# Regrouping the weight sums and the factor terms of a fast-matrix-product feed-forward stage

## The chip, the cores and the metric

The kernel runs on one core of one Trainium2 chip. TensorE (PE in the profile; PEld is its weight load), VectorE (DVE), ScalarE (ACT), GpSimd (POOL) and SyncE (SP) run in parallel and meet through semaphores only; sixteen DMA engines move data between SBUF and device memory. The metric is the device time of the kernel in microseconds (us), as the median of several executions.

## The reference

One decoder layer is applied to a prompt of 1024 tokens and to 8 single sample tokens, all with 1024 features in float32:

```python
x = x + W_out [conv(h); gla(h)],   h = rms_norm(x) @ w_in      # conv taps and a gated linear attention
x = x + cross_attn(rms_norm(x), memory K, V)                   # 4 heads, 256 memory tokens
x = x + relu(rms_norm(x) @ w_up) ** 2 @ w_down                 # 1024 -> 4096 -> 1024
y = rms_norm(x)
```

The outputs are y, the states of the convolution and of the linear attention, and the memory's keys and values. The change touches the last matrix products (w_up and w_down), what prepares them, and the times at which some transfers for them are made.

## The kernel before

Features lie on the 128 partitions, and the T = 1032 tokens along the free dimension. Every product is made in three matmuls of rounded parts (high by high, high by low, low by high), so each weight block needs a "high" copy, made by ScalarE, and a "low" rest, made by VectorE or GpSimd, and so does each moving operand.

**Tiles.** The program is numbered in weight tiles t: 16 for the memory's keys and values, 21 for the input projection (from T_IN = 16), 8 for the output projection (T_OUT = 37), 8 for the queries (T_XQ = 45), and from T_XO = 53 those of the attention's output: two over all tokens, then twelve half tiles (XO_HALVES), six for the tokens of half 0 and six for half 1. `load_w` (line 635) loads one weight tile of 512 KB on SP's queue, `w_high` (L1022) and `lo` (L902) split it. The half tiles' matmuls are at L2205; `residual_half` on VectorE (L2845) adds the result to x in `x_res` and frees the PSUM bank; its counterpart on ScalarE (L1494) squares it and `square_half` (L2851) adds the square to the norm's sum. The bank of half tile j is used again by half tile j + 2.

**Steps.** The feed-forward stage is 64 steps s: half 0 of the tokens in steps 0 to 31, half 1 in 32 to 63; within a half four groups of 4 up steps and 4 down steps. A step is a product of 2 x 2 blocks by the fast scheme with seven products instead of eight (L2264): 84 matmuls of 128x258. Its seven weight operands are A11, A12, A22 and four sums S1 to S4 of weight blocks. The moving operand has seven parts too: four quarter blocks B and three combinations T. For up steps they are the "factors" in `u_f32`/`u_op`: `factors(half, k)` scales x by the norm (two instructions, L2858) and makes the combinations (L2860, L2861, L2862), `factor_high` on ScalarE (L1519) and `factor_rest` on VectorE (L2866) split them. For half 0 they are made between the half tiles; for half 1 in steps 28 to 31 (SWITCH = 28), the last down steps of half 0.

**Weight pairs.** Two weight operands make a pair j of 512 KB. `load_pair` (L794, SP's queue) loads it into a ring of six; it waits until the product that last used the place is done. ScalarE (`comb_top`, L1527) and VectorE (`low_pair`, L2875) split it. Per step there are 3.5 pairs.

**Sums.** The sums S1 to S4 are made by DMA in device memory: SP copies a block, a GpSimd-issued DMA adds another to it (accumulate). The eight groups g have 1 MB for each sum. Groups 0 to 5 are made between tiles, from `SUM_START`, by `copy_sums` (L658, L660, L663, L666) and `add_sums` (L910, L913, L916, L919). Groups 6 and 7 ("late") are made in pieces of 256 KB in the steps that `LATE_SUMS` names: for each group six rows, (copy of S1 and S3, their add, copy of S2, add, copy of S4, add), each with the step of its four pieces. SP's copies (L674, L675, L679, L683) stand behind its pair loads, which the products release; GpSimd's adds (L986, L987, L991, L995) wait only for the first copy phase:

```python
if phases[1][p] == s:
    if p == 0:
        wait_copied(gp, g, 8)
    gp.dma_start(sum_piece(g, "S1", p), block_piece(g, "A21", p), accum_op=ALU.add)...
```

Group g is used in steps 4g to 4g + 3 and again 32 steps later. In each step ScalarE first does the rest of the step before, then `copy_first` (L1535, after the step's first product; the fifth product waits for it), then the step's comb_tops. Each engine does its instructions in order.

## Time and profile before

| what | value |
|---|---|
| time, median of 3 runs | 1449.14 us (1445.93 to 1452.72) |
| the profiled execution's own time | 1448.39 us |
| its span, first to last instruction | 1446.7 us |
| mean granted TensorE clock | 0.984 of full speed |
| PE busy | 1378.8 us, 95% |
| DVE busy | 1035.6 us, 72% |
| ACT busy | 743.3 us, 51% |
| POOL busy | 317.3 us, 22% |
| DMA | 268.25 MB, 185 GB/s in the mean |

The span is 1.7 us shorter than the execution's time; differences in the span are taken as differences in the time. A busy PE is modelled, so the lost time is better read from the length of a step than from PE's busy share: step s begins where ScalarE's `copy_first(s)` starts, step 0 at 739.2 us, step 28 at 1048.4, step 32 at 1103.4 and step 56 at 1346.1.

A row of the windows view gives a stretch, its length in us, then the busy us (and number of instructions) of PE, PEld, DVE, ACT and POOL, and last the granted clock, the DMA engines' busy share and GB/s.

### The profile page before, as it was taken

The page shows a single profiled execution, that of the slowest core. Times are in us where ns is not written, and L with a number is a line of the kernel's source. Part 1 is how long each engine was busy: PE and PEld are TensorE (multiplying, and loading weights), DVE is VectorE, ACT ScalarE, POOL GpSimd, SP SyncE. Part 2 cuts the span into 40 slices and gives each one's busy share as a digit, 9 for nine tenths or more (in the row PEclk, how much of TensorE's full clock was granted, in tenths as well). Part 3 has the DMA queues.
Part 4 walks back from the last instruction along what each step waited for, and adds up shares of the span by engine and source line. Part 5 has one row for each costly group of instructions (what it writes and reads, how often), then busy time and mean ns, then how long its engine had stood idle before and what let it go on. Part 6 is the DMA issues. An engine that isn't in the chain of part 4 may idle for free.

```text
span 1446.7 us, 25804 instructions
## 1 busy us (share of the span) xinstructions
PE 1378.8 (95%) x10477; PEld 1341.1 (93%) x10477; DVE 1035.6 (72%) x1403; ACT 743.3 (51%) x1063; POOL 317.3 (22%) x264
## 2 busy tenths in 40 slices
PE   7899999999999899999999989989997999999997
PEld 7799999998999899979898889989987999999997
DVE  5619999886533455624887678776898888798884
ACT  7561254448523333413465465554745757575674
POOL 6736495125342111104401010100000000000000
PEclk9999999999999999999999899999999999999998
DMA  9976796562595822493158788777544555666652
GB/s 355 306 173 204 174 162 150 154 121 74 198 301 179 235 74 63 153 361 117 59 190 220 232 236 238 233 209 217 180 160 132 183 183 164 199 194 210 198 167 60
DMA packets 137093, 268.25 MB, mean 185 GB/s; under 512 B 16840, under 2 KB 31496, under 8 KB 135312
## 3 DMA queue, kind: packets, MB, share of 16 engines
q1 hardware_dynamic: 119696, 233.04, 49.3%
q0 software_dynamic: 17280, 33.56, 13.3%
q8 instruction: 84, 1.38, 0.4%
q14 instruction: 33, 0.27, 0.1%
HBM read 254.26 MB, written 79.41 MB: 231 GB/s over the span
## 4 chain that ended last, share of the span: by engine, by line
PE 67%; DVE 15%; DMA 7%; ACT 6%; issue 3%; POOL 1%; SPq 0%; DVEq 0%; ACTq 0%; POOLq 0%
PE ps L2264 29%; DVE ps L2477 7%; PE ps L1806 6%; PE ps L1693 6%; PE ps L2100 6%; PE m L2264 5%; DMA raw_a<-sums 3%; PE ps L2205 3%; DMA w_raw<-in_wt 2%; PE m L1774 2%; PE ps L2134 1%; PE ps L2053 1%; PE m L2013 1%; DVE u_f L2858 1%; DVE u_op L2866 1%
## 5 line engine op out<-in xcount | busy, mean ns | idle before, releaser
L902 POOL TENSOR_TENSOR w_split<-w_raw,w_split 128x512 fp32r<-128x512 f32 x114 | 161.4, 1467 | 392.5 <-ACT w_split L1022 392.4
L1806 PE MATMUL ps<-a_op,w_split 128*128 128x344 f32 x1440 | 235.2, 323 | 4.0 <-ACT a_lr L1160 4.0
L1806 PEld LDWEIGHTS ps<-a_op,w_split 128*128 128x128 f32 x1440 | 229.1, 190 | 4.6 <-ACT a_lr L1160 4.2
L1527 ACT ACTIVATE comb_a<-raw_a 128x1024 fp32r<-128x1024 f32 x148 | 153.4, 1053 | 117.1 <-DMA raw_a<-in_wt 73.0
L2264 PE MATMUL ps<-d_op,comb_a 128*128 128x258 f32 x1512 | 196.4, 287 | 9.9 <-ACT p L1535 4.9
L2264 PE MATMUL ps<-u_op,comb_a 128*128 128x258 f32 x1512 | 191.6, 284 | 14.3 <-DVE u_op L2866 5.4
L2264 PEld LDWEIGHTS ps<-d_op,comb_a 128*128 128x128 f32 x1512 | 189.5, 192 | 12.7 <-issue 6.8
L2264 PEld LDWEIGHTS ps<-u_op,comb_a 128*128 128x128 f32 x1512 | 185.7, 190 | 16.7 <-issue 6.6
L2875 DVE TENSOR_TENSOR comb_a<-raw_a,comb_a 128x1024 fp32r<-128x1024 f32 x148 | 179.8, 1219 | 1.8 <-ACT comb_a L1527 1.7
L2477 DVE SCALAR_TENSOR_TENSOR ps<-conv_in,par,ps 128x1024 f32<-128x1024 f32 x103 | 133.0, 1291 | 3.3
L1693 PE MATMUL ps<-a_op,w_split 128*128 128x344 f32 x576 | 91.5, 320 | 0.0
L1693 PEld LDWEIGHTS ps<-a_op,w_split 128*128 128x128 f32 x576 | 90.6, 188 | 0.5 <-issue 0.5
L1022 ACT ACTIVATE w_split<-w_raw 128x1024 fp32r<-128x1024 f32 x58 | 61.0, 1052 | 51.9 <-PE ps L2205 22.4
L2100 PE MATMUL ps<-b_op,w_split 128*128 128x344 f32 x504 | 83.0, 321 | 0.0
L2100 PEld LDWEIGHTS ps<-b_op,w_split 128*128 128x128 f32 x504 | 79.7, 188 | 0.4
L2205 PE MATMUL ps<-a_op,w_split 128*128 128x258 f32 x576 | 72.5, 288 | 4.8 <-DVE x_res L2845 4.8
L2205 PEld LDWEIGHTS ps<-a_op,w_split 128*128 128x128 f32 x576 | 71.6, 194 | 5.5 <-DVE x_res L2845 5.4
L2958 DVE TENSOR_TENSOR d_op<-d_f,d_op 128x1806 fp32r<-128x1806 f32 (+2 forms) x40 | 63.7, 1609 | 6.4 <-ACT d_op L1569 6.4
L1527 ACT ACTIVATE comb_b<-raw_b 128x1024 fp32r<-128x1024 f32 (+1 forms) x38 | 39.6, 1041 | 44.5 <-DMA raw_b<-in_wt 23.0
L1569 ACT ACTIVATE d_op<-d_f 128x1806 fp32r<-128x1806 f32 (+2 forms) x40 | 53.9, 1368 | 12.2 <-DVE d_f L2948 12.2
L2264 PE MATMUL ps<-u_op,comb_c 128*128 128x258 f32 x396 | 51.0, 283 | 1.0 <-ACT p L1535 0.6
L2264 PE MATMUL ps<-u_op,comb_b 128*128 128x258 f32 x396 | 51.6, 285 | 0.0
(367 smaller groups left out, 2357.5 us busy)
## 6 DMA issues: line engine op xcount, KB each, us to landing
raw_a<-sums SPq DMA_DIRECT2D x167, 256.0 KB, 3.0
raw_a<-in_wt SPq DMA_DIRECT2D x129, 256.0 KB, 3.0
w_raw<-in_wt SPq DMA_DIRECT2D x59, 512.0 KB, 4.4
sums<-in_wt POOLq DMA_DIRECT2D x24, 1024.0 KB, 13.9
sums<-in_wt SPq DMA_DIRECT2D x12, 1024.0 KB, 10.0
sums<-sums SPq DMA_DIRECT2D x12, 1024.0 KB, 6.6
raw_c<-sums SPq DMA_DIRECT2D x43, 256.0 KB, 3.0
raw_b<-sums SPq DMA_DIRECT2D x42, 256.0 KB, 3.0
```

The lines of the kernel that those rows point to most:

```text
L902: gp.tensor_tensor(split(t, slot)[:, 1, part, :], src, split(t, slot)[:, 0, part, :].bitcast(F32), ALU.subtract).then_inc(w_low_done, 1)
L1022: act.activation(split(t, slot)[:, 0, :, :], src, ACT.Copy).then_inc(w_high_done, 1)
L1527: act.activation(pair_of(j)[0][:, 0:n_, 0], pair_of(j)[1][:, 0:n_, 1], ACT.Copy).then_inc(comb_high, 1)
L1569: act.activation(d_op[:, m, 0, f, :], d_f32[:, m, 1, f, :], ACT.Copy).then_inc(factors_high, 1)
L1693: last = pe.matmul(ps[:, c0 // CB, 0:w], w_split[:, slot, wp, k, :], src[:, k, xp, c0:c0 + w], start=(k == 0 and j == 0), stop=(k == KT - ...
L1806: last = pe.matmul(PS[0][:, b, 0:CB], w_split[:, p % 2, wp, k, :], a_op[:, k, xp, b * CB:(b + 1) * CB], start=(k == 0 and j == 0), stop=(k ...
L2100: last = pe.matmul(PS[0][:, b, 0:CB], w_split[:, t % 2, wp, k, :], b_op[:, k, xp, b * CB:(b + 1) * CB], start=(k == 0 and j == 0), stop=(k ...
L2205: last = pe.matmul(PS[bank_of(t)][:, b, 0:Q], w_split[:, t % 2, wp, k, :], a_op[:, k, xp, c0:c0 + Q], start=(k == 0 and i == 0), stop=(k = ...
L2264: last = pe.matmul(SETS[s % 2][BANK[i]][:, 0:Q], weights[:, wp, k, :], op[:, k, xp, FACTOR[i], :], start=(i < 4 and k == 0 and j == 0), st ...
L2477: link(dve.scalar_tensor_tensor(out=conv_acc, in0=src, scalar=t_, in1=conv_acc, op0=ALU.mult, op1=ALU.add))
L2875: dve.tensor_tensor(c[:, 0:n_, 1], raw_[:, 0:n_, 1], c[:, 0:n_, 0].bitcast(F32), ALU.subtract).then_inc(comb_low, 1)
L2958: dve.tensor_tensor(d_op[:, m, 1, f, :], d_f32[:, m, 1, f, :], d_op[:, m, 0, f, :].bitcast(F32), ALU.subtract).then_inc(factors_low, 1)
```

## The change

It has four parts.

1. Groups 0 to 4 of the sums are begun 3 tiles later (`SUM_TIMES` in place of `SUM_START`), group 5 up to 11 tiles later, its last add at t = 64.
2. GpSimd waits, in every step of half 0, for that step's first product before it issues its adds; before, all adds of a phase could go as soon as its copies had landed. The steps of the late groups are set anew. Both groups' first copies are now in steps 1 to 4.
3. The factors of half 1 are made early and kept in device memory. SP saves half 1 of x (`spill_rows`, before and in step 0). VectorE scales x in place in steps 6, 7, 13 and 14 (`scale_half`) and makes the combinations into `spare` in steps 15, 21, 22 and 23 (`terms_of`). ScalarE's queue stores the seven parts in the step after each (`store_terms`, four DMAs). SP loads them into `u_f32` at steps 28 and 29 (`load_terms`) ahead of these steps' pair loads, and loads x again ahead of those of step 31. `factors(1, k)` goes; `factor_high(1, 3)` moves from step 32 to 31; `factor_rest(1, k)` stays.
4. Between the half tiles, `residual_half(j)` stands ahead of `factors(0, k)` on VectorE and of `factor_high` on ScalarE from j = 7 on; `low_pair(2)` and `comb_top(2)` stand one place earlier.

```diff
@@ -100,9 +100,12 @@
-SUM_START = [T_IN - 6 + 6 * g for g in range(6)]
-LATE_SUMS = {6: ((0, 1, 2, 3), (4, 5, 6, 7), (8, 9, 10, 11), (12, 13, 14, 15), (16, 16, 17, 17), (19, 19, 20, 20)),
-             7: ((4, 5, 6, 7), (8, 9, 10, 11), (12, 13, 14, 15), (16, 17, 18, 19), (20, 20, 21, 21), (23, 23, 24, 24))}
+SUM_TIMES = [[T_IN - 3 + 6 * g + d for d in (0, 1, 2, 3, 7, 8, 12, 13)] for g in range(5)]
+SUM_TIMES.append([T_XQ + 5, T_XQ + 6, T_XQ + 7, T_XQ + 8, T_XO + 4, T_XO + 6, T_XO + 9, T_XO + 11])
+SCALE_AT = (6, 7, 13, 14)
+TERMS_AT = (15, 21, 22, 23)
+LATE_SUMS = {6: ((1, 2, 3, 4), (5, 6, 7, 8), (10, 10, 11, 12), (13, 13, 14, 14), (16, 17, 17, 17), (19, 19, 20, 20)),
+             7: ((1, 2, 3, 4), (9, 10, 11, 12), (14, 15, 15, 15), (17, 18, 18, 19), (21, 21, 21, 21), (22, 23, 24, 25))}
@@ -384,7 +387,9 @@
+        terms_loaded = x_reloaded[0]
...
+        terms_stored = x_spilled
@@ -619,6 +624,7 @@
+        terms = nc.dram_tensor("terms", (KT // 2, P, 7, Q), F32, kind="Internal").ap()
@@ -650,18 +656,17 @@
-                for g in range(len(SUM_START)):
-                    at_ = t - SUM_START[g]
-                    if at_ == 0:
+                for g, times in enumerate(SUM_TIMES):
+                    if t == times[0]:
...
-                    elif at_ == 1:
+                    if t == times[1]:
...
-                    elif at_ == 7:
+                    if t == times[4]:
...
-                    elif at_ == 12:
+                    if t == times[6]:
@@ -800,11 +805,32 @@
                 load_w(t, t % 2)
                 copy_sums(t)
 
-            for j in range(2, 4):
-                load_pair(j)
+            def spill_rows(k):
+                rows, c = slice(k, k + 5, 4), half_cols(1)
+                sp.wait_ge(ps_free, T_XO + 2 + (KT - 2) + k + 3 if k < 3 else T_SPLIT)
+                sp.dma_start(x_spill[:, rows, c], x_res[:, rows, c]).then_inc(x_spilled, 16)
+
+            load_pair(2)
+            spill_rows(0)
+            spill_rows(1)
+            load_pair(3)
+            def load_terms(k):
+                sp.dma_start(u_f32[:, k, 1, :, :], terms[k]).then_inc(terms_loaded, 16)
+
             for s in range(N_ST):
+                if s in (SWITCH, SWITCH + 1):
+                    if s == SWITCH:
+                        sp.wait_ge(terms_stored, 16 * (KT + 4) + 64 * (KT // 2))
+                        sp.wait_ge(product_done, 7 * SWITCH)
+                    for k in range(2 * (s - SWITCH), 2 * (s - SWITCH) + 2):
+                        load_terms(k)
+                if s == SWITCH + 3:
+                    sp.dma_start(x_res[:, :, half_cols(1)], x_spill[:, :, half_cols(1)]).then_inc(x_reloaded[2], 16)
                 for j in PAIRS[s]:
                     load_pair(j)
+                if s == 0:
+                    spill_rows(2)
+                    spill_rows(3)
                 copy_late_sums(s)
                 for i, at_step in enumerate(SCALE_STEPS):
                     if s == at_step + 1:
@@ -903,18 +929,17 @@
-                for g in range(len(SUM_START)):
-                    at_ = t - SUM_START[g]
-                    if at_ == 2:
+                for g, times in enumerate(SUM_TIMES):
+                    if t == times[2]:
...
-                    elif at_ == 3:
+                    if t == times[3]:
...
-                    elif at_ == 8:
+                    if t == times[5]:
...
-                    elif at_ == 13:
+                    if t == times[7]:
@@ -978,6 +1003,7 @@
                 add_sums(t)
                 lo(t, t % 2)
             for s in range(N_ST // 2):
+                gp.wait_ge(product_done, 7 * s + 1)
                 for g, phases in LATE_SUMS.items():
                     for p in range(KT // 2):
                         if phases[1][p] == s:
@@ -1515,7 +1541,10 @@
-                act.wait_ge(u_raw, 4 * half + k + 1)
+                if half == 0:
+                    act.wait_ge(u_raw, k + 1)
+                else:
+                    act.wait_ge(terms_loaded, 16 + 16 * 2 * (k // 2 + 1))
@@ -1525,6 +1554,13 @@
+            def store_terms(k):
+                act.wait_ge(u_raw, 4 + 8 + k + 1)
+                act.dma_start(terms[k, :, B11, :], x_res[:, k, HT:HT + Q]).then_inc(terms_stored, 16)
+                act.dma_start(terms[k, :, B21:B22 + 1:B22 - B21, :], halves2(x_res[:, k + 4, half_cols(1)])).then_inc(terms_stored, 16)
+                act.dma_start(terms[k, :, T4, :], spare[:, 1, :]).then_inc(terms_stored, 16)
+                act.dma_start(terms[k, :, T1:T2 + 1, :], spare[:, 2:5, :]).then_inc(terms_stored, 16)
@@ -1607,16 +1643,16 @@
             residual_half(6)
             factor_high(0, 0)
             half_weights(7)
+            residual_half(7)
             factor_high(0, 1)
-            residual_half(7)
             half_weights(8)
+            residual_half(8)
             factor_high(0, 2)
-            residual_half(8)
             half_weights(9)
+            residual_half(9)
             factor_high(0, 3)
-            residual_half(9)
+            comb_top(2)
             residual_half(10)
-            comb_top(2)
             comb_top(3)
             residual_half(11)
 
@@ -1628,14 +1664,16 @@
                     relu_last(s - 1)
                 if s - 1 >= LAST_STEP - 3:
                     end_square(s - 1)
-                if s == SWITCH + KT // 2:
-                    factor_high(1, 3)
                 copy_first(s)
+                if s - 1 in TERMS_AT:
+                    store_terms(TERMS_AT.index(s - 1))
                 if after_up and p == 0:
                     hidden_top(s - 1, "sums")
                     hidden_top(s - 1, "rest")
                 if SWITCH < s < SWITCH + KT // 2:
                     factor_high(1, s - SWITCH - 1)
+                if s == SWITCH + 3:
+                    factor_high(1, 3)
                 if s in SUM_STEPS:
                     final_square(2 * (s - SUM_STEPS[0]))
                 if after_up and p:
@@ -2861,6 +2899,26 @@
+            def scale_half(k):
+                if k == 0:
+                    dve.wait_ge(x_spilled, 16 * (KT + 4))
+                    dve.wait_ge(rstd_ready, 5)
+                r = halves2(rstd[:, half_cols(1)])
+                for m in (k, k + 4):
+                    x = halves2(x_res[:, m, half_cols(1)])
+                    dve.scalar_tensor_tensor(out=x, in0=x, scalar=par[:, G_FF + m:G_FF + m + 1], in1=r,
+                                             op0=ALU.mult, op1=ALU.mult).then_inc(u_raw, 1)
+            def terms_of(k):
+                dve.wait_ge(u_raw, 4 + 8 + k)
+                if k >= 1:
+                    dve.wait_ge(terms_stored, 16 * (KT + 4) + 64 * k)
+                top, low = halves2(x_res[:, k, half_cols(1)]), halves2(x_res[:, k + 4, half_cols(1)])
+                link(dve.tensor_tensor(spare[:, 3, :], top[:, 1, :], low[:, 1, :], ALU.subtract))
+                link(dve.tensor_tensor(spare[:, 4, :], spare[:, 3, :], top[:, 0, :], ALU.subtract))
+                link(dve.tensor_tensor(spare[:, 2, :], top[:, 0, :], top[:, 1, :], ALU.subtract))
+                dve.tensor_tensor(spare[:, 1, :], low[:, 0, :], spare[:, 4, :], ALU.add).then_inc(u_raw, 1)
@@ -2908,6 +2966,8 @@
+                if s == N_ST // 2 + KT // 2:
+                    dve.wait_ge(x_reloaded[2], 32)
@@ -2987,22 +3047,22 @@
             residual_half(6)
             factors(0, 0)
             square_half(6)
+            residual_half(7)
             factors(0, 1)
-            residual_half(7)
             factor_rest(0, 0)
             square_half(7)
+            residual_half(8)
             factors(0, 2)
-            residual_half(8)
             factor_rest(0, 1)
             square_half(8)
+            residual_half(9)
             factors(0, 3)
-            residual_half(9)
             factor_rest(0, 2)
             square_half(9)
             residual_half(10)
             factor_rest(0, 3)
+            low_pair(2)
             square_half(10)
-            low_pair(2)
             residual_half(11)
             square_half(11)
             low_pair(3)
@@ -3055,8 +3115,11 @@
                 if s in SCALE_STEPS:
                     final_scale(2 * SCALE_STEPS.index(s))
                     final_scale(2 * SCALE_STEPS.index(s) + 1)
-                if SWITCH <= s < SWITCH + KT // 2:
-                    factors(1, s - SWITCH)
+                for k in range(KT // 2):
+                    if s == SCALE_AT[k]:
+                        scale_half(k)
+                    if s == TERMS_AT[k]:
+                        terms_of(k)
             add_c21(LAST_STEP - 1)
             x_rest(LAST_STEP - 1)
```

## Rows read from the trace of the kernel before

**Rows 1.** The page: DMA's busy tenths in 40 slices of 36 us.

```profile
DMA  9976796562595822493158788777544555666652
```

**Rows 2.** The page: the chain that ended last, by engine.

```profile
PE 67%; DVE 15%; DMA 7%; ACT 6%; issue 3%; POOL 1%; SPq 0%; DVEq 0%; ACTq 0%; POOLq 0%
```

**Rows 3.** Windows: steps 0 to 27, steps 28 to 31, steps 32 to 55.

```profile
739.20:1048.40 309.20, 291.23 (x2345) 287.13 (x2344) 235.55 (x346) 182.35 (x251) 26.76 (x32) 0.98 0.75 222
1048.40:1103.40 55.00, 44.38 (x351) 42.85 (x350) 50.93 (x73) 23.46 (x26) 0.00 (x0) 0.97 0.41 134
1103.40:1346.10 242.70, 242.66 (x1998) 241.97 (x1998) 208.75 (x311) 153.83 (x211) 0.00 (x0) 0.99 0.59 190
```

**Rows 4.** Windows of single steps: 4, 5, 12, 13, 18, 19 and 54.

```profile
778.60:794.70 16.10, 13.22 (x108) 12.82 (x106) 8.98 (x14) 4.96 (x8) 6.71 (x8) 1.00 0.91 205
794.70:810.00 15.30, 12.00 (x84) 11.64 (x84) 8.13 (x12) 8.41 (x10) 0.00 (x0) 0.88 1.01 325
...
877.40:889.70 12.30, 12.29 (x100) 11.90 (x99) 8.99 (x14) 4.81 (x7) 2.38 (x3) 1.00 1.01 245
889.70:896.80 7.10, 7.01 (x59) 6.84 (x58) 6.47 (x10) 4.64 (x6) 0.00 (x0) 1.00 0.80 257
...
939.90:954.10 14.20, 12.37 (x103) 12.16 (x101) 8.74 (x12) 7.64 (x12) 3.02 (x4) 1.00 1.02 250
954.10:964.20 10.10, 8.57 (x67) 8.24 (x68) 9.32 (x14) 8.91 (x14) 0.00 (x0) 1.00 0.44 152
...
1326.80:1335.70 8.90, 8.90 (x76) 8.90 (x76) 7.95 (x14) 3.55 (x5) 0.00 (x0) 1.00 0.85 274
```

**Rows 5.** Source L794, pair loads issued from 739 to 778, then from 780 to 812.

```profile
DMA to landing us min/median/max: 2.5/3.2/5.3
...
DMA to landing us min/median/max: 2.5/7.2/15.3
```

**Rows 6.** Waits in steps 0 to 27: who waited for whom, us, times, longest.

```profile
PE ps L2264 <- ACT p L1535: 13.4, 6, 3.4
```

**Rows 7.** Groups by form, VectorE, 1048 to 1104: busy us, mean ns.

```profile
L2866 DVE TENSOR_TENSOR u_op<-u_f,u_op 128x1806 fp32r<-128x1806 f32 x4 | 8.1, 2033 | 0.7 <-ACT u_op L1519 0.7
L2858 DVE SCALAR_TENSOR_TENSOR u_f<-x_res,par,rstd 128x516 f32<-128x516 f32 x8 | 6.0, 753 | 0.1
L2860 DVE TENSOR_TENSOR u_f<-u_f 128x516 f32<-128x516 f32 x4 | 2.8, 698 | 0.1
...
L2862 DVE TENSOR_TENSOR u_f<-u_f 128x258 f32<-128x258 f32 x4 | 1.7, 428 | 0.1
```

**Rows 8.** Timelines of PE and VectorE, 694 to 742: start, us, and the idle time before.

```profile
710.61 6.07 PE L2205 MATMUL ps<-a_op,w_split 128*128 128x258 f32 x48 [0.60 <-DVE x_res L2845]
718.76 6.06 PE L2205 MATMUL ps<-a_op,w_split 128*128 128x258 f32 x48 [2.09 <-DVE x_res L2845]
726.92 7.55 PE L2205 MATMUL ps<-a_op,w_split 128*128 128x258 f32 x48 [2.10 <-DVE x_res L2845]
...
729.34 0.69 DVE L2845 TENSOR_TENSOR x_res<-x_res,ps 128x516 f32<-128x516 f32 x1
```

**Rows 9.** Timelines of SP, ACT and PE around the first input tiles.

```profile
47.78 0.57 SPq L658 DMA_DIRECT2D sums<-in_wt  x1
...
66.74 1.06 ACT L1022 ACTIVATE w_split<-w_raw 128x1024 fp32r<-128x1024 f32 x1 [9.93 <-DMA w_raw<-in_wt]
...
70.59 10.27 PE L1806 MATMUL ps<-a_op,w_split 128*128 128x344 f32 x48 [4.00 <-ACT a_lr L1160]
```

**Rows 10.** The chain that ended last, piece by piece: start, us, what.

```profile
52.72 14.00 DMA w_raw<-in_wt
...
288.22 3.78 PE ps L1806 x24
...
1100.24 2.05 DVE u_op L2866
```

**Rows 11.** The chain that ended last in 0 to 240, by line.

```profile
by line: DVE ps L2477 41.7%; DMA w_raw<-in_wt 13.2%; PE ps L1806 9.0%; POOL w_split L902 4.2%; issue 2.7%; ACT a_op L1089 2.5%; DMA m_raw<-in_mem 2.2%; POOL w_split_more L902 2.1%; DVE ps L2475 1.7%; ACT w_split L1022 1.6%; DVE rstd L2488 1
```

## The prediction

> **What bounds the kernel now.** I read the page first, then the chain that ended last, then the lengths of the steps. The chain gives two thirds of the span to PE, 15% to VectorE and 7% to DMA [rows 2], so a gain must come from stretches in which PE does not set the pace. The step length finds them. Steps 32 to 55 take 242.7 us, 10.11 us each, and PE is busy in all of it [rows 3]: this is a clean step. Steps 0 to 27 take 309.2 us where 28 clean steps are 283.1, so 26.1 us are lost. Steps 28 to 31 take 55.0 us for 40.4, so 14.6 us are lost [rows 3].
>
> The first loss lies where GpSimd's adds go out in a burst. Step 4 takes 16.1 us and step 5 15.3 us, with DMA at 0.91 and 1.01 of its capacity [rows 4]. The pair loads that land in 3.2 us in steps 0 to 3 need 7.2 us there, and up to 15.3 [rows 5]. ScalarE, which works in order, stands at a comb_top, copy_first comes late, and PE waits for it: 13.4 us in six waits [rows 6]. The second loss is VectorE's: in steps 28 to 31 it is busy 50.93 us, more than four clean steps have [rows 3], and the chain runs through its u_op [rows 10].
>
> Two smaller stretches follow. Between the half tiles PE waits for VectorE's residual three times, 0.60, 2.09 and 2.10 us, and starts its tiles 8.16 us apart, of which it works 6.06 [rows 8]. At the start, DMA is at 0.9 of capacity or so in the first slices [rows 1]; the tile load issued at 52.72 (t = 17) stands in SP's queue behind a 1 MB copy issued at 47.78, lands 14.0 us later [rows 10], and ScalarE sits idle 9.93 us and PE 4.00 us before the next work [rows 9].
>
> **The late sums (part 2).** The same 32 adds and 32 copies are made; only the time of issue changes. How much a burst costs is read from three of them: eight adds with four copies beside them (steps 4 and 5) lost 31.4 - 20.2 = 11.2 us; five adds (steps 18 and 19) lost 24.3 - 20.2 = 4.1 us; four adds (steps 12 and 13) lost nothing, 19.4 us for 20.2, though DMA was at 1.01 and 0.80 [rows 4]. After the change no step issues more than three adds; steps 5 to 12 have two each. The loss grows faster than the number, and four cost nothing, so most of the 26.1 us goes. I leave 3 us for the steps in which adds and copies meet (10, 17, 19). Bounds: 0 us left, by the four-add row, and 13 us, half of it, if it is the sum of DMA work that counts. Copies in steps 1 to 4 double to four a step; they stand behind a step's pair loads, and only the first load of the next step queues behind them. I take **-23.1 us**.
>
> **The factors of half 1 (part 3).** Taken from VectorE in steps 28 to 31: eight scalings at 753 ns (6.0 us), four instructions at 698 ns (2.8), and eight at 428 ns (3.4) [rows 7], 12.2 us. What is left is 50.93 - 12.2 = 38.7 us for 40.4. Behind the last factors(1, 3) ScalarE's split and the 2.05 us u_op on the chain [rows 10] were bare; the split is now made in step 31, and factor_rest(1, 3) runs while PE makes the first three quarters of four products. So nearly the whole 14.6 us goes; with VectorE at 96% I leave 2 us. Bounds 0 and 6 us. **-12.6 us**.
>
> The work comes back elsewhere: two scalings, 1.5 us, in each of steps 6, 7, 13, 14, and four instructions of 428 ns, 1.7 us, in 15, 21, 22, 23. VectorE is busy 8.4 us per step in steps 0 to 27 (235.55/28) and 8.7 in 32 to 55 [rows 3], and down steps have less than the mean (7.95 us in step 54 [rows 4]); these all are down steps, so 9.5 us fit under 10.11. Cover gone, it would cost 12.9 us. ScalarE issues four DMAs in each of steps 16, 22, 23 and 24; no row shows it issuing one, SP's take up to 0.57 us [rows 9], so 2.3 us a step beside 6.5 us of work (182.35/28): hidden; bare, 9 us; below nothing it cannot go, since ScalarE stored nothing before. Behind these four stand its comb_tops. Transfers: 4 x 516 KB saved, 4 x 903 KB stored and loaded, 2.1 MB reloaded, 11.4 MB in all, 35 us of the engines at 325 GB/s [rows 4]. At steps 28 and 29 SP's queue holds 1.8 MB (5.6 us) ahead of the pair loads, and 2.1 MB ahead of step 31's. ScalarE would stand for that long at comb_top; in down steps it has about half a step free, and a pair is loaded ten products, 14.4 us, before PE wants it: 14.4 - 3.2 - 5.6 leaves 5.6 us for two splits of some 1.2 us. Step 54, with 516 KB stores beside it, was at 0.85 and lost nothing [rows 4]. I allow **+3 us** for all of it, bounds 0 and 11.
>
> The Trainium skill, page "DMA: Bandwidth & Descriptors", section "Issuing engines are not separate DMA queues", says that transfers started by any engine run on the same 16 DMA engines and interleave, and that another issuing engine only saves sequencer time. By it ScalarE's queue shields nothing: 3.6 MB of stores would take their turn among the pair loads. The trace bears the rule out for GpSimd's queue, whose adds slow SP's loads from 3.2 to 7.2 us [rows 5]. As a result of its own it is rival C.
>
> **The half tiles (part 4).** VectorE's work is the same; only the residual comes ahead of the factors. PE's tiles then follow each other at about 6.1 us instead of 8.16, so half tile 11 no longer ends at 734.5 (726.92 + 7.55) but, 2 x 2.1 us of waits and 1.5 us of its slow run earlier, at about 729 [rows 8]. The first step needs the residual of half tile 10 as well. Ahead of it VectorE has the same work in both orders, so it is done at 730.0, as before [rows 8]; that sets the start. The first step begins at 730.0, not 734.4: **-4.4 us**. Bounds: the waits alone, 4.8 us, and 1 us, if the last square or low_pair, which VectorE does not end much sooner, hold the first step.
>
> **The earlier groups (part 1).** Without the copy ahead of it, tile 17's load lands some 8 us sooner, so the 4.00 us of PE's idling go [rows 9]. The 48 matmuls behind it took 10.27 us [rows 9] where 24 take 3.78 later [rows 10], so 2.7 us more are to be had. The adds now meet these loads instead, and cost something: **-6 us** of 6.7. Bounds 0 and -8. From there VectorE's tap products carry the chain without a gap, 41.7% of the first 240 us [rows 11], so the shift stays. Group 5's DMAs fall where DMA's share is 1 to 5 tenths [rows 1]: nothing.
>
> **Sum.** 1448.4 (the profiled execution's own time; the median is 0.7 higher) - 23.1 - 12.6 + 3 - 4.4 - 6 = 1405.3 us. I forecast **1405**, its own range 1396 to 1415.
>
> **Rivals.**
>
> A, forecast: 60%.
>
> B, the late sums' loss only spreads, because the same DMA work meets loads in more steps; for it, DMA is already at 0.75 in steps 0 to 27 [rows 3]; against it, the four-add row. Half of 26.1 stays: 1405 + 10 to 20 = 1415 to 1425. 18%.
>
> C, the stores and loads of the terms delay pairs at steps 16, 22 to 24, 28, 29 and 31 by their whole length, some 11 us: 1405 + 8 = 1413 to 1416. 8%.
>
> D, the early move gives nothing, since the adds now fall on tiles 16 to 18: 1411. 8%.
>
> E, slower: DMA is full in thirteen steps (1 to 4, 10, 17, 19, 22 to 24, 28, 29, 31), and each loses what steps 4 and 5 lost on average, 5.6 us: 73 us. All that can be gained is 26.1 + 14.6 + 4.4 + 6 = 51 us, so 1470; it decides from the eleventh such step. Against it, no step gets more than three adds. 5%.
>
> F, no change, with gains and new waits level: 1%.
>
> **Range and chances.** 1394 to 1427 takes in A, C, D and nearly all of B, with the leftover losses at 0 at the low end, and leaves out E. Half a per cent, 7 us, is about what a measurement here can tell from no change: faster 0.93, same 0.02, slower 0.05.
>
> **What would show it.** Steps 4, 5, 8 and 9 at 10 to 11 us; pair loads at 3 to 5 us throughout; VectorE under 40 us in steps 28 to 31, which take about 42; no u_op wait at step 32; the half tiles' matmuls 6.1 us apart; VectorE's first tap product some 6 us earlier. Wrong it would be if ScalarE stands at comb_top for much of a step after the term loads, or if GpSimd's held adds delay SP's next copies, which wait for them ahead of pair loads.

## The result

The changed kernel takes 1411.57 us (median of 4 runs, 1409.88 to 1416.01), the one before beside it 1448.28 us (4 runs). The ratio is 0.9748, with an interval from 0.9714 to 0.9781: faster by 36.7 us. The forecast was 1405 us, so the sum was 6.6 us too low. The profiled execution took 1410.50 us with a span of 1408.8 us, 37.9 less than the span of before, 1446.7.

The page of the changed kernel, the chain by engine, to be laid beside [rows 2]:

```profile
PE 70%; DVE 12%; ACT 6%; DMA 4%; issue 3%; POOL 3%; SPq 1%; DVEq 0%; ACTq 0%; POOLq 0%
```

PE has 70% of the chain instead of 67%, DMA 4% instead of 7%, VectorE 12% instead of 15%. The windows of the same kernel, steps 0 to 27 and 28 to 31, answer to [rows 3], and its steps 4 and 5 to [rows 4]:

```profile
724.70:1020.80 296.10, 287.13 (x2339) 283.31 (x2338) 248.07 (x372) 181.97 (x251) 26.46 (x32) 0.99 0.84 248
1020.80:1064.90 44.10, 42.72 (x352) 42.18 (x351) 39.19 (x53) 23.94 (x25) 0.00 (x0) 1.00 0.83 298
...
765.80:775.40 9.60, 9.19 (x74) 8.80 (x73) 8.39 (x14) 4.96 (x8) 0.00 (x0) 1.00 0.64 220
775.40:791.50 16.10, 13.80 (x115) 13.60 (x114) 8.53 (x13) 8.44 (x11) 3.35 (x4) 1.00 1.03 280
```

The 37.9 us of the span divide at these marks. Step 0 begins at 724.7 instead of 739.2: 14.5. Steps 0 to 27 take 296.1 instead of 309.2: 13.1. Steps 28 to 31 take 44.1 instead of 55.0: 10.9. What lies behind takes 343.9 instead of 343.3: -0.6. So steps 0 to 27 still lose 296.1 - 283.1 = 13.0 us, and step 5 is as long as it was (16.1 us for 15.3).

The pair loads of the changed kernel (source L799), issued from 725 to 765 and from 780 to 815, answer to [rows 5]:

```profile
DMA to landing us min/median/max: 2.6/3.9/6.0
...
DMA to landing us min/median/max: 2.6/4.1/6.8
```

Its waits in steps 0 to 27 (engine and line, what it waited for, us, times, longest) answer to [rows 6]:

```profile
PE ps L2302 <- ACT p L1571: 2.8, 1, 2.8
```

The loads behind the old burst land in 4.1 us instead of 7.2, those ahead of it in 3.9 instead of 3.2; PE's waits for ScalarE fell from 13.4 us to one of 2.8. The burst is gone, and a little of it is now everywhere.

The timeline of the changed kernel's PE at the half tiles and at the first step answers to [rows 8]:

```profile
684.63 26.41 PE L2243 MATMUL ps<-a_op,w_split 128*128 128x258 f32 x216
712.07 6.02 PE L2243 MATMUL ps<-a_op,w_split 128*128 128x258 f32 x48 [1.03 <-POOL w_split L928]
719.09 1.33 PE L2302 MATMUL ps<-u_op,comb_b 128*128 128x258 f32 x9 [1.00 <-issue]
```

Four and a half tiles run in one piece, and PE reaches the first step 1 us after the last tile: the three waits are gone.

### The same steps on PE

The marks so far are those of `copy_first` on ScalarE, which follows PE and can come late. PE's own first matmuls of step 0 (before), of steps 28, 32 and 36 before, and of steps 28, 32 and 36 after, from the timelines of PE:

```profile
734.32 1.24 PE L2264 MATMUL ps<-u_op,comb_b 128*128 128x258 f32 x9
...
1045.05 1.61 PE L2264 MATMUL ps<-d_op,comb_a 128*128 128x258 f32 x12
...
1092.34 1.34 PE L2264 MATMUL ps<-u_op,comb_a 128*128 128x258 f32 x9 [0.73 <-DVE comb_a L2875]
...
1140.37 1.61 PE L2264 MATMUL ps<-d_op,comb_b 128*128 128x258 f32 x12
```

```profile
1017.55 1.61 PE L2302 MATMUL ps<-d_op,comb_a 128*128 128x258 f32 x12
...
1058.41 1.24 PE L2302 MATMUL ps<-u_op,comb_a 128*128 128x258 f32 x9
...
1100.62 1.60 PE L2302 MATMUL ps<-d_op,comb_b 128*128 128x258 f32 x12
```

Step 0 begins 15.2 us sooner (719.09 for 734.32). Steps 0 to 27 take 298.5 us instead of 310.7, steps 28 to 31 take 40.9 instead of 47.3, and steps 32 to 35 take 42.2 instead of 48.0. From there to step 56 both kernels need the same 203.8 us, 10.19 a step, and what lies behind is 1.9 us longer (104.4 for 102.5). That last stretch takes 102.5 to 105.4 us in the profiles of all the kernels here, with no edit in it. So a good part of what the marks show as lost in steps 28 to 31 lies in steps 32 to 35: at step 32 PE has made three quarters of several products before it finishes the first, and the mark waits for the first.

### The granted clock

The mean granted clock rose too, from 0.984 of full speed to 0.992. TensorE stood at the lower of its two levels (1.2 GHz, 0.50 in the rows, instead of 2.4) in short stretches. In the kernel before they begin at 69.2, 492.4, 728.0, 796.2, 809.9 and 1100.0 us, 34 us together; in the changed one at 486.1 and 793.3, 7 us together; each kernel has one more in its last 15 us. Two windows of before, then one of the changed kernel:

```profile
809.90:816.70 6.80, 6.18 (x29) 6.21 (x30) 4.49 (x8) 3.32 (x5) 0.00 (x0) 0.50 0.23 80
1100.00:1106.80 6.80, 4.46 (x20) 4.46 (x21) 4.70 (x6) 1.54 (x3) 0.00 (x0) 0.50 0.26 77
```

```profile
793.30:796.70 3.40, 3.23 (x16) 2.96 (x16) 2.42 (x5) 2.12 (x2) 0.00 (x0) 0.51 0.10 37
```

Each of the eight stretches begins within, or up to 1.4 us behind, a wait of PE of 2.1 to 6.3 us. So a wait can cost more than its length. PE was busy for 27.0 us of these stretches before and for 6.6 after; at half the rate about half of that is lost, 13.5 and 3.3 us. By this estimate some 10 of the 37.9 us are the clock's.

### The profile page after: what moved, and what is told of

Same layout as the page of the kernel before. It is cut to its first block, busy times and chain, and to the rows that moved or that the text cites. A ratio compares the mean times of both kernels' runs of the same rounds, so it can differ in the third digit from the quotient of the medians.

```text
span 1408.8 us, 25852 instructions
## 1 busy us (share of the span) xinstructions
PE 1369.1 (97%) x10477; PEld 1332.5 (95%) x10477; DVE 1032.7 (73%) x1407; ACT 744.1 (53%) x1063; POOL 315.4 (22%) x264
## 4 chain that ended last, share of the span: by engine, by line
PE 70%; DVE 12%; ACT 6%; DMA 4%; issue 3%; POOL 3%; SPq 1%; DVEq 0%; ACTq 0%; POOLq 0%
PE ps L2302 32%; PE ps L1731 6%; PE ps L1844 6%; DVE ps L2515 6%; PE ps L2138 6%; PE m L2302 6%; PE ps L2243 3%; PE m L1812 2%; PE ps L2172 1%; PE ps L2091 1%; PE m L2051 1%; DMA raw_a<-in_wt 1%; POOL w_split L928 1%; DMA raw_a<-sums 1%; PE ps L2359 1%
## 5 line engine op out<-in xcount | busy, mean ns | idle before, releaser
L1844 PEld LDWEIGHTS ps<-a_op,w_split 128*128 128x128 f32 x1440 | 226.6, 188 | 1.0 <-DVE a_op L2414 0.6
L1731 PEld LDWEIGHTS ps<-a_op,w_split 128*128 128x128 f32 x576 | 90.6, 188 | 0.5 <-issue 0.5
L2243 PEld LDWEIGHTS ps<-a_op,w_split 128*128 128x128 f32 x576 | 69.9, 190 | 1.3 <-DVE x_res L2883 1.2
L1556 ACT ACTIVATE comb_c<-raw_c 128x1024 fp32r<-128x1024 f32 x37 | 39.0, 1055 | 29.3 <-DMA raw_c<-in_wt 19.7
```

The costliest lines, as they stand in the source:

```text
L1556: act.activation(pair_of(j)[0][:, 0:n_, 0], pair_of(j)[1][:, 0:n_, 1], ACT.Copy).then_inc(comb_high, 1)
L1731: last = pe.matmul(ps[:, c0 // CB, 0:w], w_split[:, slot, wp, k, :], src[:, k, xp, c0:c0 + w], start=(k == 0 and j == 0), stop=(k == KT - ...
L1844: last = pe.matmul(PS[0][:, b, 0:CB], w_split[:, p % 2, wp, k, :], a_op[:, k, xp, b * CB:(b + 1) * CB], start=(k == 0 and j == 0), stop=(k ...
L2243: last = pe.matmul(PS[bank_of(t)][:, b, 0:Q], w_split[:, t % 2, wp, k, :], a_op[:, k, xp, c0:c0 + Q], start=(k == 0 and i == 0), stop=(k = ...
```

## The experiments

### The parts one by one

Four kernels: the kernel before with part 1, 2 or 4 alone, and the changed kernel with part 3 undone.

```
part1_alone    before + SUM_TIMES, copy_sums and add_sums by SUM_TIMES
part2_alone    before + the new LATE_SUMS, gp.wait_ge(product_done, 7 * s + 1)
part4_alone    before + the two reordered lists of half tiles (ACT, DVE)
without_part3  changed kernel - scale_half, terms_of, store_terms,
               load_terms, spill_rows and the reload of x
```

> The kernel before with part 1 alone (groups 0 to 5 of the sums moved). Theory: in the changed kernel the input tiles end 6.9 us sooner (343.1 to 336.2 us), and the key caches and keys land sooner because no 1 MB add meets them, another 3.7 us until the queries' tiles end (601.7 to 591.2). Both should appear here: 10 to 11 us faster, step 0 at about 728.7 instead of 739.2. Rival: the second piece comes from another part of the change, then 7 us and step 0 at about 732.

> The kernel before with part 2 alone (adds held to their steps, late groups' steps set anew). Steps 0 to 27 took 309.2 us before and take 296.1 in the changed kernel, where 28 clean steps are 283.1. Theory 1 (what is left of the loss is that of the sums' own transfers, two or three adds a step being enough): 295 to 297 us here too, and about 12 us faster in all. Theory 2 (what is left comes from part 3, whose scalings, combinations, saves and stores now lie in these steps): 286 to 288 us, and about 21 us faster.

> The kernel before with part 4 alone (residuals ahead of the factors between the half tiles). Theory: the half tiles end at about 729 instead of 734.5 and step 0 begins some 4 us sooner, 4 us faster. Rival: VectorE, whose work is the same, holds step 0 and its third product, and the time is within 1 us of before.

> The changed kernel without part 3 (parts 1, 2 and 4): the factors of half 1 are made in steps 28 to 31 as before, nothing is saved, stored or loaded again. Theory 1 (sums' transfers): steps 0 to 27 stay at 294 to 296 us, steps 28 to 31 are at 55 again, and the kernel is 9 to 11 us slower than the changed one, about 1421. Theory 2 (part 3's work): steps 0 to 27 fall to 286 to 288 us, and the kernel is only 1 to 4 us slower, about 1414.

Measured: part1_alone 1437.31 us, ratio 0.9923 (0.9897 to 0.9949), 11.1 below the 1448.37 of before that was run beside it; part2_alone 1435.54, 0.9914 (0.9881 to 0.9947), 12.8 below; part4_alone 1443.28, 0.9966 (0.9949 to 0.9982), 5.1 below; without_part3 1421.26, 0.9819 (0.9782 to 0.9856), 9.7 above the changed kernel. Singly they give 11.1 + 12.8 + 5.1 + 9.7 = 38.7 us, together 36.7. The sum fits, but the places do not: part1_alone begins step 0 at 732.9 us by its mark, not at the 728.7 expected, and it has 6.9 us of its gain in steps 0 to 27 (302.3 us for 309.2), which the account of the whole books to part 2; behind step 31 it is 3.2 us longer than before.

The windows of without_part3, steps 0 to 27 and 28 to 31:

```profile
722.40:1017.70 295.30, 286.87 (x2344) 283.99 (x2344) 236.43 (x348) 181.98 (x250) 26.46 (x32) 0.99 0.80 232
1017.70:1072.70 55.00, 44.37 (x352) 42.89 (x351) 50.91 (x73) 23.49 (x25) 0.00 (x0) 0.98 0.42 134
```

Without stores, spills and VectorE's extra 11.6 us (248.07 - 236.43), steps 0 to 27 take 295.3 us instead of 296.1. So part 3's work there costs 0.8 us by the marks (1.5 on PE, 298.5 less 297.0), and the other 12.2 us of loss come from elsewhere; the late sums are the first suspect. without_part3 came out as its first theory said, in these steps and in its time. The window of part2_alone's steps 0 to 27:

```profile
739.50:1031.10 291.60, 285.25 (x2345) 282.72 (x2344) 234.86 (x346) 181.97 (x251) 26.49 (x32) 1.00 0.81 235
```

It lies between what the two theories gave, while the time, 12.8 us below before, is the first one's. It also shows how far single profiles of the same late sums differ, 291.6 and 295.3; I draw nothing from 4 us between two profiles alone. The same holds for part 3's 0.8 us.

### The adds' price: all at once, and next to nothing

```
no_hold:         -                gp.wait_ge(product_done, 7 * s + 1)
tiny_late_adds:  late adds write and read 16 rows of 512 B each, not 256 KB
```

tiny_late_adds leaves out most of the addition of groups 6 and 7, so the products that use those sums are not those of the reference.

> The changed kernel without GpSimd's wait for each step's first product; the new table of steps for the late groups stays. Theory (the hold is what breaks the bursts): the copies of both groups are done in step 4, so all 16 adds of the first phase go out in one burst; steps 0 to 27 take 308 to 318 us instead of 296.1, and the kernel is 12 to 20 us slower than the changed one. Rival (the new table does it): steps 0 to 27 stay below 299 us.

> The changed kernel with the late groups' adds cut to 16 rows of 512 bytes each, so that groups 6 and 7 carry incomplete sums; count, order and waits of the adds stay, copies too. Steps 0 to 27 are 296.1 us in the changed kernel, 13.0 over clean. Theory 1a (the adds' bytes, even at two or three a step, are what slows the pair loads): 285 to 287 us. Theory 1b (the copies, the norm of half 1 in step 5 and VectorE's order do it): 291 to 295 us.

Without the wait GpSimd issues 16 adds between 779.2 and 787.1 us. Their landing (source L1011 and L1012 of no_hold), then that kernel's window of steps 0 to 27, then that of tiny_late_adds:

```profile
L1011 POOL DMA_DIRECT2D sums<-in_wt x8: 851/2999/5216, 779.2 to 786.6; - x8
...
DMA to landing us min/median/max: 6.6/17.2/25.8
...
DMA to landing us min/median/max: 7.8/18.8/28.2
...
727.00:1035.00 308.00, 291.05 (x2339) 287.87 (x2339) 248.71 (x372) 182.02 (x251) 26.83 (x32) 0.97 0.80 238
```

```profile
723.40:1010.70 287.30, 284.56 (x2345) 282.17 (x2344) 247.62 (x372) 182.33 (x252) 24.78 (x32) 1.00 0.71 228
```

no_hold takes 1423.3 us (0.9822, 0.98 to 0.9844), 11.7 above the changed kernel: with the new table of steps, the wait is what breaks the burst. How much the table gives without the wait is not shown, since this table makes 16 adds ready at once, where that of before made eight; the wait with the old table was not run. PE stands at the lower clock for 17 us of no_hold's steps 0 to 27, and for 3.4 us of the changed kernel's; by the same estimate that is 5 of the 11.9 us by which these steps are longer. In the changed kernel the pairs of adds beside steps 5 and 6 land in 5.8 to 7.8 us. With tiny adds (one run, 1400.49 us) the steps take 287.3 instead of 296.1: the bytes of the 32 adds still cost 8.8 us, 0.27 us each in the mean, though no step has more than three. The 4.2 us above 283.1 that stay are not the adds'.

The mean hides where the 8.8 us lie. By the marks steps 4 to 7 take 40.4 us with tiny adds and 44.6 in the changed kernel, so 4.2 us of the 8.8 are there, with six of the adds. PE's wait for copy_first falls from one of 2.8 us to one of 0.4, and no stretch at the lower clock follows it:

```profile
PE ps L2302 <- ACT p L1571: 0.4, 1, 0.4
```

The other 26 adds cost 4.6 us, 0.18 each.

### Step 5 by itself

The timeline of ScalarE in step 5 of the changed kernel:

```profile
785.33 1.06 ACT L1556 ACTIVATE comb_b<-raw_b 128x1024 fp32r<-128x1024 f32 x1 [3.67 <-DMA raw_b<-in_wt]
...
787.59 1.28 ACT L1536 ACT_TABLE_LOAD   x1
788.89 0.72 ACT L1536 ACTIVATE rstd<-rstd,small 128x516 f32<-128x516 f32 x1
789.63 1.28 ACT L1537 ACT_TABLE_LOAD   x1
790.92 0.63 ACT L1537 ACTIVATE rstd<-rstd 128x516 f32<-128x516 f32 x1
791.46 0.37 ACT L1571 ACTIVATE p<-ps 128x258 f32<-128x258 f32 x1
```

norm_half(1), two activations and two table loads, stands last in step 5, behind comb_tops that wait for loads, and ahead of step 6's copy_first, for which PE waits 2.8 us. norm_first moves it ahead of the comb_tops.

```
                 copy_first(s)
+                if s == KT // 2 + 1:
+                    norm_half(1)
```

> The changed kernel with the norm of half 1 (an Ln and an Exp with two table loads, 4 us on ScalarE) moved within step 5 from behind the pairs' splits to right behind copy_first, where ScalarE waits for a pair anyway. Theory (step 6's first copy waited 2.77 us for it): steps 4 to 7 fall from 44.6 to 41 or 42 us, 2 to 3 us faster. Rival (the late pairs alone hold the copy): 44 us, no change.

The same stretch of norm_first, and its window of steps 0 to 27:

```profile
775.93 1.28 ACT L1536 ACT_TABLE_LOAD   x1
...
788.06 0.37 ACT L1571 ACTIVATE p<-ps 128x258 f32<-128x258 f32 x1
```

```profile
724.40:1017.00 292.60, 286.09 (x2344) 282.54 (x2343) 247.68 (x372) 181.65 (x250) 26.46 (x32) 1.00 0.85 251
```

The four instructions now run where ScalarE otherwise stood idle for a load, and copy_first of step 6 comes at 788.06 instead of 791.46. The steps take 3.5 us less, the kernel 1407.39 us (0.9722, 0.9701 to 0.9742), 4.2 below the changed one by medians. Their intervals overlap, so the verdict rests on steps 4 to 7, where the profiles agree: 40.7 us here and 40.9 in rests_earlier (below), which has the norm in front too, but 42.7 to 45.5 in the five kernels that hold the full adds and have the norm last (the changed one, part2_alone, without_part3, reload_later and terms_by_sp), each with one wait of 2.1 to 3.2 us for ScalarE. In the changed kernel that wait of 2.8 us brought 3.4 us at the lower clock with it (793.3); norm_first has neither. norm_half(1) stood there in the kernel before too. The forecast booked the whole 11.2 us of steps 4 and 5 to the adds.

This gain and that of tiny_late_adds are in part the same. With tiny adds norm_half(1) still stands last, and the loss of steps 4 to 7 is gone all the same (40.4 us): it takes a late pair and the norm's place together, and either cure removes it. So the 3.5 us and the 8.8 us must not be added; a kernel with both edits was not run.

### Where the adds go, and fewer of them

Two kernels on top of norm_first: one moves the adds into the steps in which ScalarE has most room, up to four a step; the other takes group 6 out of LATE_SUMS and makes it among the early ones.

```
adds_in_down_steps:
+LATE_SUMS = {6: ((1, 1, 2, 3), (4, 5, 6, 7), (8, 9, 10, 11), (12, 12, 13, 13), (15, 16, 17, 18), (20, 20, 21, 21)),
+             7: ((2, 3, 4, 4), (7, 13, 14, 15), (16, 17, 18, 19), (20, 21, 22, 22), (23, 23, 23, 23), (24, 24, 25, 25))}
group6_early:
+SUM_TIMES.append([T_XQ + 6, T_XQ + 7, T_XQ + 8, T_XO + 1, T_XO + 5, T_XO + 7, T_XO + 10, T_XO + 12])
```

> norm_first with another table of late steps: all but four of the 32 late adds fall into down steps (4 to 7, 12 to 15, 20 to 23), up to four in one step; as before the copies of S2 and S4 fill the up steps between. Theory (a pair that lands late costs time only in up steps, where ScalarE and VectorE are full): steps 0 to 27 fall from norm_first's 292.6 to 288 to 290 us, 3 us faster. Rival (each add costs its 0.27 us wherever it stands, and more where three or four meet): 292 us or more.

> norm_first with group 6 of the sums made like groups 0 to 5, in eight transfers of 1 MB between tiles 51 and 65, where DMA is at 0.2 to 0.4 of its capacity, so that 16 of the 32 late adds and 16 of the 32 late copies leave the steps. Theory (what is left of the loss goes with the adds in the steps, 0.27 us each): steps 0 to 27 fall from norm_first's 292.6 to 286 to 289 us, and step 0 begins as before: 3 to 6 us faster than norm_first, 1402 to 1404. Rival (the 1 MB adds delay tile loads between the half tiles, and step 0 begins later by what the steps gain): 1406 or more.

Windows of steps 0 to 27, first adds_in_down_steps, then group6_early:

```profile
727.30:1024.70 297.40, 287.18 (x2344) 283.92 (x2343) 247.93 (x372) 182.24 (x250) 26.58 (x32) 0.99 0.83 247
```

```profile
727.80:1016.00 288.20, 284.63 (x2343) 282.14 (x2342) 248.00 (x372) 182.07 (x252) 13.21 (x16) 1.00 0.75 226
```

adds_in_down_steps takes 1414.77 us (0.9784, 0.976 to 0.9808) and its steps 4.8 us more than norm_first's. My theory fell. On PE, of the steps left without adds, 16 to 19 became clean (40.3 us for norm_first's 43.2) and 8 to 11 hardly did (42.6 for 43.6), while steps 20 to 23, with eight adds, take 46.5 us for 41.5 and steps 24 to 27, with four, 43.4 for 40.7. PE's longest wait there is 3.5 us for VectorE's spare, and 3.4 us at the lower clock follow it, at 973.3. Down steps do not take adds for nothing; that thin spreading is what counts is the reading, by this one table.

group6_early's steps take 4.4 us less than norm_first's, for 16 adds and 16 copies: 0.28 us for an add with its copy. That is no second measurement of tiny_late_adds' 0.27, which kept the copies and held the loss of steps 4 to 7, and 4.4 us is about what two profiles of the same late sums differ by. Its step 0 begins 3.4 us later, and its 1407.58 us (5 runs, 0.9724, 0.9711 to 0.9738) are norm_first's within their spread: not the 1402 to 1404 expected. The later start is not shown to be group 6's doing. The input tiles end 1.6 us later and the attention stage is 1.7 us longer; the first have the lower clock for 6.8 us at 222.6 where norm_first has it for 3.4, and the second has it for 3.4 us at 488.9 where norm_first has none. The first extra copy goes out at 509.27 us.

### Steps 28 to 31, and who stores the terms

What is still lost there by the marks, 44.1 - 40.4 = 3.7 us, could be the reload of x or VectorE's own work. On PE it is less: steps 28 to 31 take 40.9 us, as the clean down steps 36 to 39 do (40.8), and steps 32 to 35 lose about 1.9 us (42.2 for 40.3 in the clean up steps 40 to 43), 1.36 of it in the wait below. Timelines of VectorE, then of PE, at the start of step 32 of the changed kernel:

```profile
1062.19 2.03 DVE L2924 TENSOR_TENSOR u_op<-u_f,u_op 128x1806 fp32r<-128x1806 f32 x1
...
1064.28 0.63 PE L2302 MATMUL ps<-u_op,comb_a 128*128 128x258 f32 x3 [1.36 <-DVE u_op L2924]
```

```
reload_later:    s == SWITCH + 3  ->  s == SWITCH + 5   (the 2.1 MB reload of x)
rests_earlier:   norm_first, factor_high(1, k) and factor_rest(1, k) one step earlier each
terms_by_sp:     store_terms(k) taken from ScalarE, its four DMAs issued by SP
                 behind the step's pair loads
```

> The changed kernel with the 2.1 MB reload of x moved from step 31 to step 33; it is needed in step 36. Theory (the reload delays the pairs of step 31, VectorE comes late with the last factor's rest, and PE waits 1.36 us for it): steps 28 to 32 fall from 52.6 to 50.5 to 51.5 us, and nothing is lost in 33 to 35: 1 to 2 us faster. Rival (VectorE's own amount of work in these steps holds it): 52 to 53 us.

> norm_first with the splits of the half 1 factors one step earlier (ScalarE's and VectorE's, two in step 29, one each in 30 and 31, none left for 32). Theory (VectorE's 2 us rest at the head of step 32 is what PE waits 1.36 us for, and step 31 is overfull): steps 28 to 32 fall from 52.5 to 51 us, 1 to 2 us faster. Rival (VectorE's total in these steps sets the time): 52 to 53 us, no change.

> The changed kernel with the terms' stores issued from SP's queue, behind the step's pair loads, and not from ScalarE's. Theory (by the skill's rule that the issuing engine only saves sequencer time, with ScalarE having time to spare in these steps): within 2 us of the changed kernel, steps 20 to 27 within 1 us of its 81.9. Rival (ScalarE's four issues, some 2 us a step, hold its comb_tops): 2 to 4 us faster. Second rival (SP must wait for VectorE's terms ahead of its next pair loads): 3 to 8 us slower.

reload_later takes 1416.57 us (0.9785, 0.9762 to 0.9808), 5.0 above by medians, with intervals that overlap. Steps 28 to 32 stay at 52.6 us and the wait of 1.36 us stays, so the reload was not its cause. The reload now costs something behind it: steps 32 to 35 take 44.6 us on PE for 42.2. That is 2.4 us; another 3.1 us of its profile lie in steps 0 to 27, which the move can't reach.

rests_earlier takes 1410.24 us (0.9749, 0.9732 to 0.9767), and its steps 28 to 31:

```profile
1020.90:1067.00 46.10, 44.35 (x352) 43.76 (x351) 39.19 (x53) 24.02 (x25) 0.00 (x0) 0.96 0.80 284
```

The same 39.19 us of VectorE, and 2.0 us longer, with a granted clock of 0.96. The u_op wait at step 32 is gone, and steps 32 to 35 are clean on PE (40.6 us). But in step 29 VectorE now makes two rests in a row (3.98 us) ahead of a low_pair, and PE waits for that pair (timeline of PE of rests_earlier):

```profile
1040.31 2.67 PE L2302 MATMUL ps<-d_op,comb_a 128*128 128x258 f32 x12 [1.74 <-DVE comb_a L2933]
```

From 1040.7 us the clock stands at 0.50 for 3.4 us, about 1.7 us more. So this order trades one wait for another and 1.7 us of clock, and its time is norm_first's within their intervals. It does not show that VectorE's total alone sets the time; an order with neither wait was not tried.

terms_by_sp takes 1419.24 us (0.9807, 0.9789 to 0.9825), 7.7 above. The first product of VectorE's terms for k = 2 in the changed kernel, and in terms_by_sp:

```profile
968.84 0.43 DVE L2917 TENSOR_TENSOR spare<-x_res 128x258 f32<-128x258 f32 x1 [1.54 <-DMA terms<-spare]
```

```profile
975.64 0.43 DVE L2922 TENSOR_TENSOR spare<-x_res 128x258 f32<-128x258 f32 x1 [5.90 <-DMA terms<-spare]
```

VectorE waits for the store that reads spare before it overwrites it. In SP's queue the store is issued only behind the pair loads, and the wait grows from 1.54 to 5.90 us. PE in turn waits 4.1 us for VectorE's spare, once, and 3.4 us at the lower clock follow; steps 20 to 27 take 87.2 us instead of 81.9. These 5.3 us are the stores'. Another 3.2 us of this profile are there before step 0 begins (722.32 on PE for 719.09), where no store is. The theory fell, and the second rival came. ScalarE's own issues of one set of stores in the changed kernel took 0.33, 0.46, 0.59 and 0.64 us, 2.0 together; the first and the last:

```profile
960.07 0.33 ACTq L1560 DMA_DIRECT2D terms<-x_res  x1
...
961.54 0.64 ACTq L1563 DMA_DIRECT2D terms<-spare  x1
```

## Why the prediction was right, and where a term was off

Taken on PE in the profiles of before, of the changed kernel and of without_part3 (part 4 from part4_alone, part 1 as the rest of the 15.2 us by which step 0 begins sooner), the terms came out so:

| term | predicted | in the profiles |
|---|---|---|
| part 2, late sums | -23.1 | -13.7 (steps 0 to 27: 310.7 to 297.0, without_part3) |
| part 3, steps 28 to 35 | -12.6 | -12.3 |
| part 3, its traffic in steps 0 to 27 | +3 | +1.5 |
| part 4 | -4.4 | -4.5 |
| part 1 | -6 | -10.7 |
| behind step 56 | none | +1.9 |
| sum | -43.1 | -37.8 |

**Late sums: right mechanism, mis-sized.** The burst went, and the pair loads with it to 4.1 us. But the step "I leave 3 us", with its ground "four cost nothing", failed: by the marks 12.2 us stayed. It had three faults. First, the four-add row was read between copy_first's marks on ScalarE, which can run late against PE. PE's own matmuls in the kernel before, the first of step 12's d_op and the first of what follows step 13, and then that which follows the clean steps 36 and 37 (which began at 1140.37):

```profile
874.15 1.61 PE L2264 MATMUL ps<-d_op,comb_b 128*128 128x258 f32 x12
...
895.19 1.59 PE L2264 MATMUL ps<-d_op,comb_c 128*128 128x258 f32 x12
...
1160.91 1.59 PE L2264 MATMUL ps<-d_op,comb_c 128*128 128x258 f32 x12
```

The two steps took 895.19 - 874.15 = 21.0 us of PE, not 19.4, and the clean pair took 20.5: four adds lost 0.5 us, not nothing. Secondly, the same trace has another burst of four, and the forecast passed it over (timeline of GpSimd):

```profile
985.85 3.36 POOL L995 DMA_DIRECT2D sums<-in_wt  x4 [42.93 <-DMA sums<-sums]
```

Steps 22 and 23, beside it, took 14.8 + 7.2 = 22.0 us by the marks, 1.8 over clean. Thirdly, part of the loss of steps 4 to 7 came from norm_half(1)'s place together with late pairs, and spreading the adds left it: moving the norm took 3.5 us. What is shown of the 12.2 us is this: 8.8 go with the adds' bytes, of which up to 4.2 go with the norm's place as well; what the other 3.4 are is open. Rival B had left 13 us of the 26.1, and 12.2 to 13.0 stayed, so in this term B was right in size, and for the adds' part in its reason too. That the kernel did not end in B's 1415 to 1425 is part 1's doing, below.

**Factors of half 1: right.** VectorE is at 39.19 us in steps 28 to 31, as forecast (38.7), and about 2 us stay on PE in steps 28 to 35, as forecast. They lie in steps 32 to 35: the u_op wait at step 32 did not vanish, it shrank from 5.40 us to 1.36. About 2 of the 12.3 us gained are the clock's, by the estimate above (the window at 1100.0).

**Traffic and ScalarE's issues.** Four issues cost ScalarE 2.0 us, for 2.3 estimated, and are hidden. Rival C did not come: the steps with terms cost 0.8 us in all by the marks and 1.5 on PE, both within what two profiles differ by. The Trainium skill, page "DMA: Bandwidth & Descriptors", section "Issuing engines are not separate DMA queues", holds that another issuing engine saves only sequencer time. What the trace shows beside it is the wait of 5.90 us in terms_by_sp: the transfers are the same, but an engine that issues in order decides when they begin, and that was worth 5.3 us in steps 20 to 27.

**Half tiles: right, and for its reason.** part4_alone begins step 0 at 729.82 us on PE, 4.5 sooner, just behind VectorE's residual of half tile 10 (729.03, 0.68 us long); 730.0 was forecast. Its time is 5.1 below before.

**Earlier groups: more than forecast, partly for another reason.** The input tiles end at 336.2 instead of 343.1, 6.9 for 6. PE's 4.00 us of idling [rows 9] are gone, as the timelines of ScalarE and PE of the changed kernel show:

```profile
60.74 1.06 ACT L1048 ACTIVATE w_split<-w_raw 128x1024 fp32r<-128x1024 f32 x1 [2.94 <-DMA w_raw<-in_wt]
```

```profile
69.48 4.53 PE L1844 MATMUL ps<-a_op,w_split 128*128 128x344 f32 x27 [0.33 <-DVE a_op L2414]
```

The 2.7 us that the forecast took from the 10.27 us of 48 matmuls [rows 9] had a cause that it did not name: from 69.2 to 76.0 us the granted clock was 0.50, and it is full there in the changed kernel.

The other 3.6 us come in the attention stage, where I looked at nothing but DMA's tenths. In the kernel before, GpSimd issued a 1 MB add at 468.07 us and SP the loads of cache_a at 468.5 and 469.0; after the change no add goes out beside them. PE ahead of the scores, and the split of the keys that it waits for on ScalarE, before and after:

```profile
495.07 4.96 PE L2013 MATMUL m<-k_op,a_op 128*128 128x256 f32 x24 [6.27 <-issue]
...
493.62 0.63 ACT L1393 ACTIVATE k_op<-k_raw 128x512 fp32r<-128x512 f32 x1 [10.21 <-DMA k_raw<-out_mk]
```

```profile
484.87 4.43 PE L2051 MATMUL m<-k_op,a_op 128*128 128x256 f32 x24 [2.87 <-issue]
...
483.41 0.63 ACT L1419 ACTIVATE k_op<-k_raw 128x512 fp32r<-128x512 f32 x1 [6.81 <-DMA k_raw<-out_mk]
```

The cache loads land in 11.0 us instead of 16.8. The keys' load, which SP issues behind them (at 482.91 us before, 476.70 after), lands in 6.7 us instead of 10.7. ScalarE's wait for it and PE's wait both fall by 3.4 us. part1_alone has this gain as well (254.5 us for this stage, 258.6 before). So rival D was wrong by the whole term.

**The errors against each other.** Late sums 9.4 us worse, part 3 0.3 worse, behind step 56 1.9 worse, part 1 4.7 better, traffic 1.5 better, part 4 0.1 better: 5.3 us, for 1410.5 - 1405.3 = 5.2. The forecast held partly because two errors of opposite sign met: part 1 gave 3.6 us from a stage that the forecast had put at nothing, and that is luck. The clock had no term; its 10 us or so are inside the others.

**Left open.** With part 1, the input tiles end anywhere from 335.4 to 341.0 us in the profiles of these kernels. The granted clock goes with it: in the changed kernel, without_part3 and tiny_late_adds they end at 335.4 to 336.2 us, and the clock is full at 220 us; in norm_first, no_hold and reload_later they end at 338.7 to 339.2, with 3.4 us at 0.50 from 223 or 224 us on; in the other five at 339.9 to 341.0, with 6.8 us at 0.50. In these eight, and in none of the three, PE had just idled 2.2 to 2.3 us for VectorE (timeline of PE of norm_first):

```profile
220.86 1.13 PE L1812 MATMUL m<-qz,k_t 128*128 128x128 f32 x8 [2.29 <-DVE sc_t L2571]
```

What makes VectorE come late there in some kernels was not tried, and these 2 to 6 us are as large as the differences among the best kernels here. Each kernel has one trace and its median several runs, so how often each falls into this is not known.

## What to carry to other kernels

Read a step's length on the engine that sets the pace, not from the mark of an engine that follows it: 1.6 us of drift turned a price into none, and at step 32 the marks put a loss into the wrong steps. Read more than one row for a price: a second burst of four adds spoke against the first. Before a burst is blamed for a slow step, look at what else stands in the in-order queue of the engine that is waited for; here four instructions ahead of one copy cost 3.5 us. When two cures reach the same wait, do not add their gains. Look at the granted clock behind each wait of PE, because a wait can cost half as much again. Background transfers are best spread as thin as they go and held to the consumer's steps, but they keep a price, so count them.

## What the runs showed of the hardware

A 256 KB add from DRAM to DRAM in GpSimd's queue landed in 5.8 to 7.8 us with one other beside it, and in up to 28.2 us when 16 were issued within 8 us. GpSimd's issue of one grew in the same burst from about 0.85 us to a median of 3.0 us (L1011). Spread to at most three a step, the bytes of 32 adds still cost 8.8 us, 4.2 of them in steps 4 to 7; an add with its copy cost 0.28 us by group6_early.

TensorE's granted clock stood at 0.50 for 3.4 or 6.8 us beside or just behind waits of PE of 1.7 to 6.3 us, in the eight stretches of the two kernels above and at 1040.7 us of rests_earlier. Twelve matmuls of 128x258 took 1.6 us at full clock and 2.9 in such a stretch (793.97 us of the changed kernel).
